# Differential attention as one run of 32 row-tile steps, scores two tiles ahead

## What is computed

```python
s = einsum('pbhid,pbhsd->pbhis', qi, k) * scale + bias      # p = 0, 1
s = where(rel >= 0, s, -inf)
p = softmax(s, axis=-1)
w = p[0] - lam * p[1]
o = einsum('bhis,bhse->bhie', w, v)                          # 128 rows i a block
o = o * rsqrt(mean(o * o) + eps) * sub_g * (1 - lam_init)    # then o @ w_out
```

## Time and profile before

| what | us |
|---|---|
| median of 3 runs | 2507.26 (2504.75 to 2509.08) |
| the profiled execution, whole | 2503.24 |
| its span, first to last instruction | 2501.6 |
| differential attention stage, 758.06 to 1072.73 | 314.67 |
| TensorE busy in that stage | 230.24 |

### The profile page before, as it was taken

How to read it: one execution, slowest core, us unless ns; L and a number is a source line. 1 busy time by engine, 2 the same in 40 slices (tenths; PEclk the granted TensorE clock), 3 DMA queues, 4 the chain that set the end, 5 groups by cost and what they waited for, 6 DMA issues and landing times. The chain is left out here.

```text
span 2501.6 us, 28004 instructions
## 1 busy us (share of the span) xinstructions
PE 2149.2 (86%) x9990; PEld 1720.7 (69%) x9990; DVE 1430.3 (57%) x1853; ACT 1066.4 (43%) x1135; POOL 353.0 (14%) x309
## 2 busy tenths in 40 slices
PE   7889899999987777589999977667782999999994
PEld 5767578888866666378888866546452888777773
DVE  3442255565344443555465345987613898888885
ACT  3325524343323334414343223133311787778773
POOL 1000100000000000100000002657101122222222
PEclk9989999999998888789999998878885999999997
DMA  7221029432224111114332223211014999999995
GB/s 205 68 76 68 17 79 359 117 101 101 90 62 115 43 55 43 51 31 129 85 101 101 93 59 92 65 34 34 17 38 151 356 398 399 399 398 400 397 398 226
DMA packets 275831, 378.61 MB, mean 151 GB/s; under 512 B 12712, under 2 KB 174684, under 8 KB 275608
## 3 DMA queue, kind: packets, MB, share of 16 engines
q1 hardware_dynamic: 258248, 315.14, 37.5%
q0 software_dynamic: 17488, 62.19, 6.7%
HBM read 341.08 MB, written 38.84 MB: 152 GB/s over the span
## 5 line engine op out<-in xcount | busy, mean ns | idle before, releaser
L969 PE MATMUL PS<-XS,split 128*128 128x512 f32 (+1 forms) x2304 | 482.3, 372 | 3.6 <-DVE XS L152 3.1
L969 PEld LDWEIGHTS PS<-XS,split 128*128 128x128 f32 x2304 | 406.6, 189 | 79.0 <-DVE XS L152 3.6
L152 DVE TENSOR_TENSOR moe_split<-moe_raw,moe_split 128x2048 fp32r<-128x2048 f32 x174 | 398.1, 2290 | 86.0 <-ACT moe_split L147 85.8
L152 DVE TENSOR_TENSOR split<-ring,split 128x2048 fp32r<-128x2048 f32 x101 | 231.3, 2293 | 366.9 <-ACT split L147 366.7
L147 ACT CAST moe_split<-moe_raw 128x2048 fp32r<-128x2048 f32 x174 | 332.6, 1912 | 69.5 <-DMA moe_raw<-in_expert_w_gate 38.6
L2498 PE MATMUL PS<-moe_split,moe_x 128*128 128x512 f32 x1392 | 348.2, 401 | 8.0 <-DVE moe_split L152 4.8
L2498 PEld LDWEIGHTS PS<-moe_split,moe_x 128*128 128x128 f32 x1392 | 259.1, 191 | 72.0 <-DVE moe_x L152 13.0
L147 ACT CAST split<-ring 128x2048 fp32r<-128x2048 f32 x112 | 213.0, 1904 | 199.5 <-PE PS L1005 110.8
L1005 PE MATMUL PS<-split,XS 128*128 128x512 f32 x960 | 218.4, 390 | 0.3 <-DVE XS L152 0.3
L1005 PEld LDWEIGHTS PS<-split,XS 128*128 128x128 f32 x960 | 180.1, 188 | 38.3 <-issue 1.1
L2520 PE MATMUL PS<-moe_split,moe_h 128*128 128x512 f32 x696 | 164.8, 393 | 2.1 <-DVE moe_h L152 2.1
(11 more groups left out here) (346 smaller groups left out, 2657.8 us busy)
## 6 DMA issues: line engine op xcount, KB each, us to landing
moe_raw<-in_expert_w_gate SPq DMA_DIRECT2D x58, 1024.0 KB, 13.8
moe_raw<-in_expert_w_up SPq DMA_DIRECT2D x58, 1024.0 KB, 13.9
moe_raw<-in_expert_w_down SPq DMA_DIRECT2D x58, 1024.0 KB, 13.5
ring<-in_w_up SPq DMA_DIRECT2D x88, 512.0 KB, 5.1
ring<-in_w_down SPq DMA_DIRECT2D x44, 512.0 KB, 4.3
expert_rows<-rows POOLq DMA_DIRECT2D x4, 4096.0 KB, 30.4
expert_rows<-W POOLq DMA_DIRECT2D x29, 512.0 KB, 7.0
ring<-in_w_in SPq DMA_DIRECT2D x24, 512.0 KB, 5.3
```

The lines of the kernel that those rows point to most:

```text
L152: return dve.tensor_tensor(lo, raw, hi.bitcast(F32), ALU.subtract)
L969: mm = pe.matmul(PS[:, b + q, rows], w[:, c, q, :], x_half(k, high)[:, c, rows], start=(c == 0 and m == 0), stop=(c == KC - 1 and m == 2))
```

## The change

The stage runs as 32 steps across heads instead of 8 passes. In step n TensorE does turn_w(n), the first half of a projection, score(n+2), value(n) and the second half of the projection. A half of q or k is four of the eight chunks of the contraction; a half of a v turn is one of its two row tiles. q of the next head stands in step 4h, k in 4h+1, the two halves of v in 4h+2 and 4h+3. `turn_y` of head h-1 closes step 4h+2. ScalarE and VectorE get the matching order. The copies of `squares` become one instruction, `keep_y`, at the head of step 4h, and value waits for it alone instead of for all of squares. Splits of pieces 5 to 14 stand at fixed steps (`high_at`), and `piece_used` becomes one semaphore for each split slot, since k of one head now ends before v of the pair; the even layer and the feed-forward take the same helper. The wait of `turn_w` for `y_out` goes from i = 2 to i = 3. No arithmetic changes.

```diff
@@ piece_high @@
-        act.wait_ge(k.piece_used, n - SPLIT + 1)
+        act.wait_ge(k.piece_used[piece_slot(k, n)], n // SPLIT)
@@ new @@
+def piece_done(k, instruction, n):
+
+    instruction.then_inc(k.piece_used[piece_slot(k, n)], 1)
@@ diff_stage: order of the projections @@
+    fill = {n: [] for n in range(N)}
+
+    def put(step, turn):
+        turns.append(turn)
+        fill[step[0]].append((len(turns) - 1, 0))
+        fill[step[1]].append((len(turns) - 1, 1))
+
+    for h in range(HD - 1):
+        for i, part in enumerate("qk"):
+            put((4 * h + i, 4 * h + i), (DIFF_PIECES.index(("qk", h + 1)), part, h + 1))
+        if h < HD - 2:
+            put((4 * h + 2, 4 * h + 3), (DIFF_PIECES.index(("v", h // 2 + 1)), "v", h // 2 + 1, h % 2))
...
-    follows = {u: n + SPLIT for n, u in lasts.items()}
+    high_at = {2: 5, 8: 6, 9: 7, 10: 8, 16: 9, 17: 10, 18: 11, 24: 12, 25: 13, 26: 14}
@@ tensor: turn_w, value, turn_y @@
-            if i == 2:
+            if i == 3 and h > 0:
                 pe.wait_ge(y_out, h)
...
-                pe.wait_ge(squared, h)
+                pe.wait_ge(y_kept, h)
...
-            pe.wait_ge(w_out, min(4 * h + 6, 4 * HD))
+            pe.wait_ge(w_out, min(4 * h + 7, N))
@@ tensor: order @@
-        for h in range(HD):
-            pe.wait_ge(kept, k_kept[h])
-            score(h, 0)
-            score(h, 1)
-            if h > 0:
-                turn_w(h - 1, 3)
-                value(h - 1, 3)
-            project(after[h][0])
-            turn_w(h, 0)
-            score(h, 2)
-            value(h, 0)
-            turn_w(h, 1)
-            score(h, 3)
-            project(after[h][1])
-            if h > 0:
-                turn_y(h - 1)
-            value(h, 1)
-            turn_w(h, 2)
-            project(after[h][2])
-            value(h, 2)
-        turn_w(HD - 1, 3)
-        value(HD - 1, 3)
+        project(0, 0)
+        project(0, 1)
+        project(1, 0)
+        project(1, 1)
+        project(2, 0)
+        score(0)
+        score(1)
+        project(2, 1)
+        project(3, 0)
+        project(3, 1)
+        for n in range(N):
+            turn_w(n)
+            for u, part in fill[n][:1]:
+                project(u, part)
+            if n + 2 < N:
+                score(n + 2)
+            value(n)
+            for u, part in fill[n][1:]:
+                project(u, part)
+            if n % 4 == 2 and n > 4:
+                turn_y(n // 4 - 1)
         turn_y(HD - 1)
@@ scalar: order @@
+        keep(0)
+        keep(1)
+        rows(0)
+        rows(1)
+        piece_high(k, act, 3)
+        keep(2)
+        keep(3)
+        piece_high(k, act, 4)
+        for n in range(N):
+            h, i = divmod(n, 4)
+            leave_w(n)
+            if i == 1 and h > 0:
                 root(h - 1)
+            if n + 2 < N:
+                rows(n + 2)
+            for u, part in fill[n]:
+                if part == 1:
+                    keep(u)
+            if i == 2 and h > 0:
                 leave_y(h - 1)
+            if n in high_at:
+                piece_high(k, act, high_at[n])
+            if n == 4 * EARLY + 2:
                 act.wait_ge(projected, len(turns))
                 act.drain()
                 act.copy(x_half(k, 1)[:, 0:EARLY, :], YT[:, 0:EARLY, :]).then_inc(early_high, 1)
@@ vector: keep_y split off from squares, order @@
-            for t in range(NT):
-                dve.tensor_copy(on[:, t, :], PS[:, 5, t * P:(t + 1) * P])
+            dve.tensor_copy(on, PS[:, 5, :].rearrange("p (t n) -> p t n", t=NT)).then_inc(y_kept, 1)
...
+        add_bias(0)
+        add_bias(1)
+        piece_low(k, dve, 3)
+        mix(0)
+        piece_low(k, dve, 4)
+        for n in range(N):
+            h, i = divmod(n, 4)
+            if i == 0 and h > 0:
+                keep_y(h - 1)
+            if n + 1 < N:
+                mix(n + 1)
+            if n + 2 < N:
+                add_bias(n + 2)
+            if i == 0 and h > 0:
                 squares(h - 1)
+            if i == 1 and h > 0:
                 norm(h - 1)
+            if n - 1 in high_at:
+                piece_low(k, dve, high_at[n - 1])
+            if i == 2 and h - 1 >= EARLY:
                 low_y(h - 1)
```

More of the change, by code:

```diff
@@ L181, in piece_ready, with pieces_in_slot @@
     pe.wait_ge(k.freed[slab[0]], slab[1] + 1)
+def piece_done(k, instruction, n):
+    instruction.then_inc(k.piece_used[piece_slot(k, n)], 1)
+def pieces_in_slot(k, slot):
+    return sum(piece_slot(k, n) == slot for n in range(len(k.pieces)))
 def piece_halves(k, n, chunks):
@@ L974, in tensor @@
     def tensor(pe):
-        pe.drain().then_inc(k.piece_used, 1)
+        piece_done(k, pe.drain(), len(k.pieces) - 1)
         for turn in range(2):
@@ L1244, in diff_stage @@
     EARLY = 6
+    N = 4 * HD
     turns = [(0, "q", 0), (0, "k", 0), (1, "v", 0, 0), (1, "v", 0, 1)]
-    after = {}
-    for h in range(HD):
[L1249 to L1260, removed]
+    fill = {n: [] for n in range(N)}
[8 more added lines that the diff above has]
+            put((4 * h + 2, 4 * h + 3), (DIFF_PIECES.index(("v", h // 2 + 1)), "v", h // 2 + 1, h % 2))
+    lasts = {turn[0]: u for u, turn in enumerate(turns)}
     k_kept = [1 + turns.index((DIFF_PIECES.index(("qk", h)), "k", h)) for h in range(HD)]
     v_kept = [1 + lasts[DIFF_PIECES.index(("v", p))] for p in range(HD // 2)]
-    follows = {u: n + SPLIT for n, u in lasts.items()}
+    high_at = {2: 5, 8: 6, 9: 7, 10: 8, 16: 9, 17: 10, 18: 11, 24: 12, 25: 13, 26: 14}
     def sync(sp):
@@ L1297, in project @@
                     for m, (w, high) in enumerate(((wh, 1), (wh, 0), (wl, 1))):
-                        mm = pe.matmul(PS[:, bank, :], w[:, c, part], x_half(k, high)[:, c, :],
+                        mm = pe.matmul(PS[:, bank, :], w[:, c, columns_], x_half(k, high)[:, c, :],
                                        start=(c == 0 and m == 0), stop=(c == KC - 1 and m == 2))
             else:
[L1301 to L1313, removed]
+                t = 2 * turns[u][3] + part
+                for c in range(KC):
+                    for m, (high, w) in enumerate(((1, wh), (1, wl), (0, wh))):
+                        mm = pe.matmul(PS[:, bank, 256 * part:256 * part + 256],
+                                       x_half(k, high)[:, c, t * P:(t + 1) * P], w[:, c, :],
+                                       start=(c == 0 and m == 0), stop=(c == KC - 1 and m == 2))
@@ L1314, in score @@
+            if part == 1:
+                mm.then_inc(projected, 1)
+                if lasts[n] == u:
+                    piece_done(k, pe.drain(), n)
+        def score(n):
+            h, i = divmod(n, 4)
             b = n % 2
+            if i == 0:
+                pe.wait_ge(kept, k_kept[h])
             if n >= 2:
@@ L1392, in keep, with rows @@
                     .then_inc(kept, 1)
[L1393 to L1398, removed]
+        def rows(n):
+            L = (n % 4 + 1) * P
             act.wait_ge(negated, n + 1)
@@ L1427, in scalar @@
         piece_high(k, act, 2)
[L1428 to L1437, removed]
-                root(h - 1)
[L1439 to L1443, removed]
+        keep(0)
[7 more added lines that the diff above has]
+        for n in range(N):
+            h, i = divmod(n, 4)
+            leave_w(n)
+            if i == 1 and h > 0:
+                root(h - 1)
+            if n + 2 < N:
+                rows(n + 2)
+            for u, part in fill[n]:
+                if part == 1:
+                    keep(u)
+            if i == 2 and h > 0:
                 leave_y(h - 1)
-            leave_w(h, 2)
-            keep(after[h][2])
-            if h == EARLY:
+            if n in high_at:
+                piece_high(k, act, high_at[n])
+            if n == 4 * EARLY + 2:
                 act.wait_ge(projected, len(turns))
@@ L1480, in mix, with keep_y @@
                                      ALU.mult, ALU.add).then_inc(mixed, 1)
-        def squares(h):
+        def keep_y(h):
             dve.wait_ge(valued, 4 * h + 4)
@@ L1506, in low_y @@
             split_low(dve, PS[:, 4, :], x_half(k, 1)[:, h, :], x_half(k, 0)[:, h, :]).then_inc(y_out, 1)
[L1508 to L1517, removed]
+        for n in (1, 2):
             piece_low(k, dve, n)
@@ L2837, in odd_block @@
             k.pieces, k.piece_shift = k.odd_pieces, 2
-            k.piece_highs, k.piece_used = k.sem("odd_piece_highs"), k.sem("odd_piece_used")
+            k.piece_highs = k.sem("odd_piece_highs")
+            k.piece_used = [k.sem(f"odd_piece_used{i}") for i in range(SPLIT)]
             yield diff_stage(k)
```

81 lines of the change are left out of this document (31 added, 50 removed).

## The result

| | us |
|---|---|
| before, median of 4 runs | 2507.5 (2504.8 to 2509.1) |
| changed, median of 4 runs | 2430.7 (2428.6 to 2432.5) |
| ratio | 0.9694, 95% interval 0.9678 to 0.9711 |
| forecast | 2436 (2425 to 2467) |
| span of the profiled execution, before and changed | 2501.6 and 2427.0 |

The account below looks back on a forecast made before the run. The prediction took TensorE's waits for one tile's chain, 84.4 us idle, plus 29 us of half clock as the stage's bound. Gains of 66.5 and 4.6 us, 71 together, gave 2507.3 - 71 = 2436 us, range 2425 to 2467.

Parts of the forecast that it names:

- Head: One head in the new steps: 26.6 us at full clock, against 37.4 before.
- leave_y 1.18 a head: turn_w(i=3) directly behind turn_y needs leave_y out of bank 4: TensorE stands 1.05 us a head.
- the v pieces: Heads 2 and 4: the v projection waits for its piece's late low half, 1.15 us, twice.
- Opening: First four projections stay at 24.56 us, with scores 0 and 1 inside; TensorE comes to step 0 at 783.5.
- Last projection: End of the last projection in the stage: 959.1 instead of 1025.6, 66.5 us less.
- 17.35 + 7.8: TensorE's work in one head at full clock: 17.35 us of projections and 7.8 us of small groups.
- Tail: Last projection's end to first output product: 42.5 us instead of 47.1, 4.6 less; range of gain 0 to 6.
- Sum: Whole gain: 66.5 us up to the last projection plus 4.6 in the tail, 71 us.
- Given back later: Rival: output product or feed-forward waits for late pieces or loads, about 2480 us; chance 0.04.
- Rivals of a mixed or half clock: Mixed: clock 0.84 in heads 0 to 5, 2466 us, chance 0.08. Half clock for two thirds: 2562, chance 0.04.
- waits for mix in the middle heads: Sign of wrong VectorE order: waits of 1 us or more; rival that half the waits stay, 2467 us, chance 0.11.
- These are waits for the chain of one tile: TensorE's 63.3 us of turn_w waits for mix and 10.2 for leave_w put down to score, add_bias, exponential, mix, turn.

Follow-up runs that it names:

- Experiment 5: Changed kernel with turn_y ahead of value, leave_y ahead of the exponentials and v pieces split one place earlier: 2419.3 us, ratio 0.9656.
- Experiment 6: Changed kernel with later splits of pieces 13 and 14, a later copy of six heads and its low half on VectorE: 2422.3 us, ratio 0.9674.
- experiment 1: Kernel before, with only each low half of a weight piece moved behind the mix it stood in front of on VectorE: 2460.4 us, ratio 0.9824.
- (10): Changed kernel with each low half in front of mix on VectorE, as the kernel before had it: 2442.8 us, ratio 0.9764.
- (2): Changed kernel with scores one tile ahead instead of two, on all three engines: 2497.8 us, ratio 0.9974.
- (3): Changed kernel with each projection whole between turn_w and score instead of in two halves: 2450.6 us, ratio 0.9780.
- (4): Changed kernel with value of tile 4h waiting for all of squares, squares directly behind keep_y: 2434.0 us, ratio 0.9716.
- experiments 8 and 9: Kernel before with 12 useless matmuls at each of twelve places (8) or six long waits (9): 2509.6 us, ratio 1.0016, and 2497.2 us, ratio 0.9973.

## Why the prediction was right, point by point

- *Head.* Head 1 took 26.26 us against 26.6, at clock 1.00 as assumed. leave_y 1.18 a head against 1.05, the v pieces 1.10 and 1.11 against 1.15. Experiment 5 shows that these terms were on the path.
- *Opening.* Step 0 at 784.23, 783.7 if the stage's start, 0.54 later here, is taken off; the forecast was 783.5.
- *Last projection.* It ended at 956.85; the forecast was 959.1, which is 2.8 us too late once the stage's later start is taken off. Heads 1 to 5 make 1.6 of that, head 0 and steps 24 and 25 some 0.7 each. In head 1 the error is TensorE's busy time, 24.71 us where 17.35 + 7.8 had 25.15; the idle time was forecast to 0.1 us.
- *Tail.* 41.6 against 42.5, and for the reasons given: high pieces and the copy in front of leave_w (1.63 and 2.78 us), GpSimd's hold (3.22 us before turn_w of tile 29). Experiment 6 took 6 us out of it. GpSimd held VectorE until 975.03, 18.2 us after the last projection, where the walk had 17.8, and keep_y was not held.
- *Sum.* 74.8 against 71 in the stage; 2.8 of the difference are the steps' and 0.9 the tail's. Given back later: nothing. Rivals of a mixed or half clock: the clock was 1.00; waits for mix in the middle heads: none.
- *What was wrong is the reading of why.* "These are waits for the chain of one tile" holds for a third of the 63.3 us at most (the 22.8 of experiment 1). Experiment 1 shows that moving the splits alone brings 44 us, more than half of the 77; the prediction listed the splits among what "can" hold the chain and put the waits down to the chain. The number was right, as I see it, since the walk through the new steps held the splits, the mixes and the copies in their new order, whatever the cause had been. The rival that was missing is "the splits' new place does most of it".
- *Two readings of rows.* "Nine tenths busy or more in most of the kernel" is 20 slices of 40 in the earlier trace rows. Of the four windows for the small groups "at clock 1.00" the third, 0.55 us, stands at 0.50 in the earlier trace rows; three turns at full clock take 0.52 (849.62 in the changed kernel), so the sum is not touched.
- *The parts do not add.* Splits alone 44 us (1), the pipeline with the splits in front of mix 59 (10), both 77. The lead hides most splits, and moved splits leave only the chain to the lead. But the lead of two tiles cannot be spared (2), the halves are worth 21 us (3), keep_y little (4).

What stays open: how much of the 76.8 us the higher clock brought by itself, beside the stops that went. The busy time fell by 20.9 us, but stops and clock went together, and experiments 8 and 9 show only that the clock is a cost of its own (11.3 and 7.2 us of busy time there), not its share here. The semaphore for each split slot was not run by itself.

## What to carry to other kernels

Before a wait is put down to a chain, look what stands in front of the late instruction on its own engine: here a split of weights for a later stage, itself waiting for the projection just done, made two thirds of the waits for mix (40.5 of 63.3 us), and moving it by one place gave more than half of what the whole pipeline gave. Lay out a new order as a table of one period, each engine in its queue order with durations from the trace: it gave the stage to 4 us of 240, and the small stops that it showed (five of 1.2 and two of 1.1 us) could be taken out one for one. Keep the lead longer than the chain plus what queues in front of it, on every engine of the chain, and lay long fillers in halves around the short dependent groups.

## What the runs showed of the hardware

GpSimd and VectorE can each hold the other: GpSimd's subtraction started 0.9 us before VectorE's ended and took 7.43 us instead of 6.66; then a 128x256 VectorE scale took 4.11 us instead of 0.34 and ended with GpSimd, while a PSUM copy (0.69 us, as long as the one at 991.66, where GpSimd does nothing), a reciprocal and a 128x1 scale on VectorE ran undisturbed. The Trainium skill, "SBUF — State Buffer", section "SBUF: two separate sides", describes an exclusive lock on a shared port pair, which only some VectorE operations take; the trace agrees, 4.11 us for the held scale and 0.69 for the copy out of PSUM. Groups of matmuls of 3 us or less, with stops of up to 1.2 us, left the clock at 1.00 for 172.77 us; the clock swinging because of frequent short idles between groups of matmuls, which the Trainium skill tells of ("TensorE: Matmul & The Clock Gate", section "A second HAM failure mode: psum-queue depth-cycling") was not seen here. Useless matmuls in place of six waits of over 4 us raised the stage's clock from 0.83 to 0.87 and made the kernel 0.27% faster.
